# RWKV projection: value slabs last, and head sums as two rounded products

## The reference, cut to what matters

```python
rkvg = einsum('bsmd,mde->bsme', xs[:, :, :4], w_in)     # xs = h + xx * mu, one mix per matrix
r, k, v, g = rkvg[:, :, 0], rkvg[:, :, 1], rkvg[:, :, 2], rkvg[:, :, 3]
kk = heads(k * k_k)
kk = kk / maximum(sqrt(sum(kk * kk, axis=-1)), 1e-12)     # key norms: sums over a head
k_dir = k * (1 + (icl - 1) * k_a)                         # icl: a sigmoid, for two directions
bonus = (sum(r * k_dir * r_k, axis=-1) * v).sum(over both directions)
out = ((groupnorm(scan(r, decay, k_dir, v, kk, icl)) + bonus) * silu(g)) @ w_out
```

## Time and profile before

| what | value |
|---|---|
| median of three runs | 4685.58 us |
| the profiled execution | 4690.08 us |
| its span, first to last instruction | 4688.3 us |
| TensorE matmul busy | 4258.9 us, 91% |
| VectorE, ScalarE busy | 2696.7 us, 58%; 1887.8 us, 40% |
| mean granted TensorE clock | 0.968 |
| DMA | 480.77 MB, mean 103 GB/s |

### The profile page before, as it was taken

The page is one execution under the profiler, slowest core; times in us unless marked ns, Lnnn a source line. Parts: engine busy times, 40 slices in busy tenths (PEclk is TensorE's granted clock), DMA queues, the critical chain, the costliest instruction groups (busy, mean ns, idle before and its releaser), DMA issues. The chain is left out here.

```text
span 4688.3 us, 137401 instructions
## 1 busy us (share of the span) xinstructions
PE 4258.9 (91%) x61184; PEld 3665.6 (78%) x61184; DVE 2696.7 (58%) x4665; ACT 1887.8 (40%) x3496; POOL 4.6 (0%) x10
## 2 busy tenths in 40 slices
PE   6999979999997899999998999889999789999978
PEld 2888768888885799766668899877988678888858
DVE  5433547777775654355556433466425577777755
ACT  5333225545554432355554000154332245555542
POOL 0000000000000000000000000000000000000000
PEclk8999989999999999899999999999999899999989
DMA  7444773333325132100000221112446733333341
GB/s 294 150 123 123 223 225 87 98 83 97 87 80 192 63 84 56 51 1 2 1 10 28 95 95 68 57 52 82 117 139 195 236 110 89 98 85 96 85 183 63
DMA packets 542442, 480.77 MB, mean 103 GB/s; under 512 B 29344, under 2 KB 500640, under 8 KB 534176
## 3 DMA queue, kind: packets, MB, share of 16 engines
q1 hardware_dynamic: 411040, 405.91, 27.3%
q10 hardware_dynamic: 130816, 66.07, 5.2%
HBM read 337.94 MB, written 128.71 MB: 100 GB/s over the span
## 5 line engine op out<-in xcount | busy, mean ns | idle before, releaser
L647 PE MATMUL ps<-big_r,stage_r 128*128 128x384 f32 x2976 | 641.3, 350 | 19.1 <-DVE big_r L908 17.7
L647 PEld LDWEIGHTS ps<-big_r,stage_r 128*128 128x128 f32 x2976 | 522.6, 190 | 75.7 <-issue 27.0
L2508 PE MATMUL ps<-big_r,w_out 128*128 128x384 f32 x2304 | 417.8, 341 | 36.5 <-DVE w_out L2624 36.2
L2508 PEld LDWEIGHTS ps<-big_r,w_out 128*128 128x128 f32 x2304 | 407.7, 191 | 44.9 <-DVE w_out L2624 39.2
L647 PE MATMUL ps<-big_r,w_slab_r 128*128 128x384 f32 x1488 | 341.4, 337 | 0.0
L370 PE MATMUL ps<-big_r,stage_r 128*128 128x384 f32 x1536 | 311.7, 337 | 13.2 <-DVE big_r L357 13.2
L2230 DVE TENSOR_REDUCE extra<-ps 128x1 f32<-128x1152 f32 (+1 forms) x144 | 177.6, 1234 | 205.0 <-PE ps L2135 205.0
L370 PEld LDWEIGHTS ps<-big_r,stage_r 128*128 128x128 f32 x1536 | 270.7, 189 | 27.7 <-issue 26.7
L1491 ACT COPY arena<-ps 128x512 f32<-128x512 f32 x288 | 168.9, 587 | 253.4 <-PE ps L1294 252.9
L647 PEld LDWEIGHTS ps<-big_r,w_slab_r 128*128 128x128 f32 x1488 | 268.2, 189 | 0.0
L1645 DVE COPY_PREDICATED arena<-arena,ps 128x128 f32<-128x128 uint32 x720 | 192.9, 325 | 116.6 <-PE ps L1282 115.5
(11 more groups left out here) (259 smaller groups left out, 8087.5 us busy)
## 6 DMA issues: line engine op xcount, KB each, us to landing
w_slab<-in_w SPq DMA_DIRECT2D x138, 512.0 KB, 3.7
scan_in<-x_resid ACTq DMA_DIRECT2D x112, 576.0 KB, 5.9
arena<-scan_in SPq DMA_DIRECT2D x144, 320.0 KB, 3.8
arena<-scan_in SPq DMA_DIRECT2D x288, 128.0 KB, 3.8
arena<-scan_in SPq DMA_DIRECT2D x48, 576.0 KB, 7.5
arena<-scan_in SPq DMA_DIRECT2D x144, 192.0 KB, 4.0
arena<-in_w_ada SPq DMA_DIRECT2D x24, 1024.0 KB, 5.8
x_resid<-in_w_ada SPq DMA_DIRECT2D x24, 1024.0 KB, 4.9
```

Source lines behind the costliest of these rows:

```text
L647: mm = pe.matmul(g.ps[:, 3 * s + c, 0:CW], w[:, k * P:(k + 1) * P], x[:, k, chunk(c)], start=k == i == 0, stop=k == NB - 1 and i == 2)
L2508: mm = pe.matmul(g.ps[:, bank(i, b), 0:wide[i]], w[:, b, k * P:(k + 1) * P], r, start=k == j == 0, stop=k == NB - 1 and j == 2)
```

## The change

The matrices' order becomes keys, receptance, gate, values: GATE = 18 and VAL = 26. The gate's sigmoid, product and store move to slabs 18 to 25. Values are the last matrix; the bonus is multiplied with the values in their copy buffer (evac), and the loads of values from memory are gone. Squares and bonus products are split into a high and a low part, and each norm and each sum is two rounded products with head_ones_r, a rounded copy of the ones. The norm of block 6 moves from slab 9 to slab 10. The first load of lora_up moves from the start to slab 12, since its place now holds the high squares. The last bonus block is copied, and multiplied by one instruction once the last values are out.

```diff
-RWKV_MATS = (..., ("value", 2, NB), ("gate", 3, NB))
+RWKV_MATS = (..., ("gate", 3, NB), ("value", 2, NB))
...
+    sq_high, sq_low = up_flat_r[:, 0:T], g.x_r[:, 4, :]
-    back = [[g.big[1][:, 2 + 3 * i + k, :] for k in range(3)] for i in range(2)]
+    back = [[g.big[1][:, 2 + 3 * i + k, :] for k in range(2)] for i in range(2)]
+    prod_low = [g.extra_r[:, 0:T], g.big_r[0][:, 0, :]]
+    prod_high = [g.big_r[1][:, 4 + 3 * i, :] for i in range(2)]
+    copies = lambda n: n + 1 if n < GATE else n + 1 - NB
...
@@ SP
-            def load_v(b):
-                sp.wait_ge(stored[b % 2], 16 * (9 + b // 2))
-                ...
-                sp.dma_start(tiled(back[b % 2][2]), blocks(b, A_V)).then_inc(v_in[b % 2], 16)
...
             def load_up(w):
                 if w:
                     sp.wait_ge(rate_mm, 2 * CH * NB)
+                else:
+                    sp.wait_ge(norm_mm, CH * NB)
...
-            load_up(0)
...
+                if n == RCP + 2:
+                    load_up(0)
+                if GATE < n <= VAL:
+                    store_gate(n - GATE - 1)
-                if n == GATE:
+                if n == VAL:
                     load_kr(0)
-                    load_v(0)
-                    slab(GATE + 2)
+                    slab(VAL + 2)
                     load_kr(1)
-                    load_v(1)
-                elif n > GATE:
-                    b = n - GATE
+                elif n > VAL:
+                    b = n - VAL
                     if b + 1 < NB:
                         load_kr(b + 1)
-                    store_gate(b - 1)
-                    if b + 1 < NB:
-                        load_v(b + 1)
                     store_bonus(b - 1)
                     if b == 4:
                         scan_head()
...
@@ TensorE
             def slab(n, m, between):
                 pe.wait_ge(low_ok, n - 2)
-                if n > GATE + 1:
-                    pe.wait_ge(silu_ok, n - GATE - 1)
+                if GATE <= n - 2 < VAL:
+                    pe.wait_ge(silu_ok, n - 2 - GATE + 1)
                 else:
-                    pe.wait_ge(copied, n - 1)
+                    pe.wait_ge(copied, copies(n - 2))
...
             def norm(b, c):
                 if c == 0:
-                    pe.wait_ge(sq_ok, b + 1)
+                    pe.wait_ge(sq_low_ok, b + 1)
...
-                pe.matmul(..., g.head_ones[:, :], sq[:, chunk(c)], start=True, stop=True).then_inc(norm_mm, 1)
+                pe.matmul(out, g.head_ones_r[:, :], sq_high[:, chunk(c)], start=True, stop=False)
+                pe.matmul(out, g.head_ones_r[:, :], sq_low[:, chunk(c)], start=False, stop=True).then_inc(norm_mm, 1)
...
             def sums(b, c):
                 if c == 0:
-                    pe.wait_ge(p_ok, b + 1)
+                    pe.wait_ge(p_low_ok, b + 1)
...
-                pe.matmul(..., g.head_ones[:, :], prod[b % 2][:, chunk(c)], start=True, stop=True).then_inc(sum_mm, 1)
+                pe.matmul(out, g.head_ones_r[:, :], prod_high[b % 2][:, chunk(c)], start=True, stop=False)
+                pe.matmul(out, g.head_ones_r[:, :], prod_low[b % 2][:, chunk(c)], start=False, stop=True).then_inc(sum_mm, 1)
...
-                if n < RCP - 1 or n == RCP + 1:
-                    q = min(n - KEY - 1, NB - 1)
+                if n < RCP - 1 or n in (RCP, RCP + 1):
+                    q = n - KEY - 1 if n < RCP else n - RCP + NB - 2
                     between = {4: (lambda q=q: norm(q, 0), lambda q=q: norm(q, 1)), 6: (lambda q=q: norm(q, 2),)}
-                elif n == RCP - 1:
-                    between = {2: (lambda: norm(NB - 2, 0), lambda: norm(NB - 2, 1)), 6: (lambda: norm(NB - 2, 2),)}
...
@@ ScalarE
             def copy_out(n):
                 act.wait_ge(proj_done, n + 1)
-                if n >= KEY + 2:
+                if n in (VAL, VAL + 1):
+                    act.wait_ge(silu_st[b % 2], 64)
+                elif n >= VAL:
+                    act.wait_ge(stored[n % 2], 16 * (NB + b // 2))
+                    act.wait_ge(bonus_ok, CH * (b - 1))
+                elif n >= KEY + 2:
                     act.wait_ge(stored[n % 2], 16 * (n // 2 - 1))
...
             def square(b):
                 A.activation(sq, evac[b % 2], ACT.Square, scale=ch(g, "k_k", 8 * j + b)).then_inc(sq_ok, 1)
+                A.activation(sq_high, evac[b % 2], ACT.Square, scale=ch(g, "k_k", 8 * j + b)).then_inc(sq_high_ok, 1)
...
-                copy_out(VAL + b)
+                gate(b)
             for b in range(NB):
                 if b < NB - 1:
                     for c in range(CH):
                         rates(NB + b + 1, c)
                         if b == c == 0:
-                            high_slab_of(GATE + 1)
-                gate(b)
+                            high_slab_of(VAL + 1)
+                act.wait_ge(p_ok, b + 1)
+                A.copy(prod_high[b % 2], prod[b % 2]).then_inc(p_high_ok, 1)
+                copy_out(VAL + b)
             for s in range(2):
                 act.wait_ge(rate_st[s], 16 * 16)
+                act.wait_ge(stored[s], 16 * 12)
...
@@ VectorE
             def bonuses(b, c):
-                    dve.wait_ge(v_in[b % 2], 16 * (b // 2 + 1))
...
+                out, sums = bonus[b % 2][:, chunk(c)], g.ps[:, bank(("sum", b, c)), 0:CW]
+                if b == NB - 1:
+                    V.tensor_copy(out, sums).then_inc(bonus_ok, 1)
+                    return
+                if c == 0:
+                    dve.wait_ge(copied, copies(VAL + b))
+                V.tensor_tensor(out, sums, evac[b % 2][:, chunk(c)], op=ALU.mult).then_inc(bonus_ok, 1)
...
+            def low_products(b):
+                dve.wait_ge(p_high_ok, b + 1)
+                V.tensor_tensor(prod_low[b % 2], prod[b % 2], prod_high[b % 2], op=ALU.subtract).then_inc(p_low_ok, 1)
+
+            def low_squares(b):
+                dve.wait_ge(sq_ok, b + 1)
+                dve.wait_ge(sq_high_ok, b + 1)
+                V.tensor_tensor(sq_low, sq, sq_high, op=ALU.subtract).then_inc(sq_low_ok, 1)
+
+            V.tensor_copy(g.head_ones_r[:, :], g.head_ones[:, :]).then_inc(ones_ok, 1)
...
                 if b == NB - 1 and m < 5:
-                    if m == 2:
-                        ... (transition(m + 1, keys_between); unit_keys(NB - 2))
+                    if m < 4:
+                        transition(m + 1, lambda k: None)
+                    else:
+                        def gate_between(k):
+                            if k == 2:
+                                gated(NB - 2)
+                        transition(m + 1, gate_between)
+                        gated(NB - 1)
                     continue
                 if m == 5:
                     if b:
                         rate_sums(b)
                     weighted_keys(b)
                     if b:
-                        gated(b - 1)
                         high_slab_of(n + 1)
                     products(b)
                     if b:
                         for c in range(CH):
                             bonuses(b - 1, c)
+                    low_products(b)
                     continue
                 if b:
                     high_slab_of(n + 1)
+                if m == 4 and b:
+                    gated(b - 1)
...
-                if KEY < n < RCP or n == RCP + 1:
-                    q = min(n - KEY - 1, NB - 1)
+                if KEY < n < RCP or n in (RCP, RCP + 1):
+                    q = n - KEY - 1 if n < RCP else n - RCP + NB - 2
+                    low_squares(q)
                     for c in range(CH):
                         maxima(q, c)
                     unit_keys(q)
...
-            gated(NB - 1)
-            dve.wait_ge(silu_ok, NB)
+            dve.wait_ge(copied, copies(W_RWKV - 1))
+            V.tensor_tensor(bonus[1], bonus[1], evac[1], op=ALU.mult).then_inc(last_ok, 1)
```

More of the change, by code:

```diff
@@ L401 @@
 ADA_WITH = ((1, 2, 3), (), (4, 5), ())
-RWKV_MATS = (("decay", 4, 1), ("rate", 5, 1), ("key", 1, NB), ("receptance", 0, NB), ("value", 2, NB), ("gate", 3, NB))
+RWKV_MATS = (("decay", 4, 1), ("rate", 5, 1), ("key", 1, NB), ("receptance", 0, NB), ("gate", 3, NB), ("value", 2, NB))
 def phase_rwkv_project(nc, g, layer, j):
@@ L432, in phase_rwkv_project @@
     first = [0, 1, 2, 10, 18, 26]
-    KEY, RCP, VAL, GATE = first[2:]
-    raw = lambda n: g.slab[:, n % 2] if n < GATE + 2 else g.big[0][:, 3 + n % 2, 0:D]
+    KEY, RCP, GATE, VAL = first[2:]
+    copies = lambda n: n + 1 if n < GATE else n + 1 - NB
+    raw = lambda n: g.slab[:, n % 2] if n < VAL + 2 else g.big[0][:, 3 + n % 2, 0:D]
     turned = [first[m] + i for m in (3, 4, 5) for i in range(2)]
@@ L438, in phase_rwkv_project @@
     V, A = nc.vector, nc.scalar
-    rates_in = dict(zip([*range(RCP + 3, RCP + 7), *range(VAL + 1, VAL + 5), VAL + 6], range(NB + 1)))
-    rates_in.update({GATE + b: NB + b + 1 for b in range(NB - 1)})
+    rates_in = dict(zip([*range(RCP + 3, RCP + 7), *range(GATE + 1, GATE + 5), GATE + 6], range(NB + 1)))
```

(19 more changed lines are left out.)

67 lines of the change are left out of this document (28 added, 39 removed).

## The result

| | median us | runs | ratio to before, 95% interval |
|---|---|---|---|
| before | 4686.63 (4680.41 to 4693.78) | 6 | |
| after | 4715.53 (4706.04 to 4721.80) | 6 | 1.0059 [1.0049, 1.0069] |
| forecast | 4680.6, range 4660 to 4702 | | 0.9989 |

The change made the kernel slower, by 28.9 us, and the time lies outside the range. The profiled execution of after took 4709.96 (span 4708.1).

What follows compares the result with a forecast made beforehand. TensorE was taken to bound the projections, hardly resting outside a few slabs. Terms summed to -2.5 us a phase, -5.0 for two: 4680.6 against the median of 4685.6, with an 8-in-10 range of 4660 to 4702.

Steps and rivals of the forecast that it cites:

- Slab 27: Gate store ahead of key and receptance loads makes them late: +2.3 us a phase, bounds 0 and +7.
- Slabs 3 to 8: Key norms as two rounded products gain 0.93 us a slab, -5.6 a phase; second square and subtraction fit in time.
- Slab 32: Rates wait for the rate store's landing, sooner with less traffic ahead: -6 us a phase, bounds 0 and -10.
- Rival C: The rate store's share of the engines is fixed, so slab 32's wait stays: +7 us, 4693; chance 0.12.
- Slabs 28 to 31: Loop over ScalarE's rounded copy and VectorE's low products sets 17.0 us a slab: -1.1 a phase, bounds -0.98 and +1 each.
- Rival B: ScalarE's queue, now issuing value stores too, becomes the bound in the last stage: +17 us, 4703; chance 0.12.
- slabs 9 and 10: Block 6's norm waits in slab 10 for the transition; TensorE rests 8.6 us, then slower clock: +9.7 a phase.
- Slabs 11: Cheaper norms -0.93 us, low squares some 0.2 late: -0.7 a phase.
- 26: Gate product added to the transition, last matrix's slab perhaps sooner: +0.4 us a phase, bounds -1 and +1.4.
- 33: Six cheaper sums, none behind the loop: -1.9 us a phase; the phase's ends +0.4, bounds -0.5 and +3.
- Rivals A: Queue relief is worth more: slab 32 falls to 17.0 in both phases, slab 27 gains 1 us: 4665; chance 0.18.
- D: The wait in slab 10 isn't there: -24 us, 4661; chance 0.04.

Runs made afterwards that it cites:

- the mended version: After with low squares ahead of the split, block 6's norm mostly in slab 9, gate store behind key loads: 0.9960, again 0.9980; with unrounded sums 0.9978.

## Why the prediction was wrong

The forecast was -5.0 for two phases and they took +28.1. Of the 33 between them:

- **Slab 27, 13.4 of it.** The mechanism was the forecast one, a store moved past loads; the term of +2.3 was mis-sized (+6.9 / +11.1), and in phase 2 its upper bound of +7 too. Counted from slab 27's start, with before's slab at 506.20 and after's at 514.6, the loads went out at 503.6 (forecast 503.5) and VectorE had them at 511.4 (forecast 510), TensorE resumed at 519.7 (518.2): 1.5 of it. The larger part is the second block, for which the forecast had "about 1.5 more". Its loads were in place 13.0 us after their issue began, where the forecast took 6.5 for a landing, while everything SP had held back was under way on full DMA engines (1.09, 322 GB/s); TensorE rested again 3.88. The rests are the loss: 4.31 us before, 7.61 and 3.88 after. The half clock behind a rest, which I priced for slabs 10 and 32 and not here, is not: before has it in slab 27 too (0.86 in the earlier trace rows), and TensorE was busy 2.9 us beyond a slab's own pace before (20.19 less 17.28) and 3.4 after (19.81 less 16.38). In phase 2 the issue and the landing were slower still (VectorE waited 8.73 and 3.69). Moving the store back took 18.0 away.
- **Slabs 3 to 8, 10.0.** The price of a norm was right: 0.93 a slab, 0.91 in slab 8 and in the 82.0 of the run with the squares first. The step that failed is "fit": the forecast let the low squares end at 6.8, from ScalarE's copy and squares and the subtraction alone, and did not list what stands ahead of the subtraction on VectorE, whose queue has 4.5 us of halving and split there. The sentence "up to 1 if they were late" held the outcome and went into neither the term nor the range.
- **Slab 32, 6.7.** Phase 1 gave 5.3 of 6; phase 2 gave nothing. From the issue of the rate store to the sigmoids that wait for it were 16.6 and 13.6 us; now 12.8 (613.55 to 626.35) and 14.4. The forecast took 5.5 from both; 3.8 came in phase 1, and 0.8 was lost in phase 2. The engines were full in this wait (1.10, 349 GB/s), so 4.5 MB passed in it, the store's own 1.18 MB among them, and which of the others the store had to let pass is not seen in a row. The run without value stores (23.7 / 24.9) says that the 0.59 MB of a value store behind it matter by under 1 us, as far as one run tells. Rival C, the fixed share, fits phase 2 and not phase 1. The Trainium skill's rule behind it (DMA: Bandwidth & Descriptors, Queues, rings and completion order: turns packet by packet between the rows that have work) was not isolated by any run here. Why the phases differ stays open.
- **Slabs 28 to 31, 4.5.** The loop was wrongly named. It is not the copy, the low products and the sums (the forecast's 17.0, and it is some 0.3 us from being the one that ends last) but the rate store's landing: 8.11 and 9.14 are 17.25. The 17.3 that TensorE itself needed before (and in the run with the sums back) are as long as that loop, so it could not be seen there, and making the sums cheaper than it could not give anything. Of the 4.5, 2.6 are slab 29, where the landing came later than in its neighbours (9.06 for 8.11 in phase 1); why is open. Rival B named the right place, ScalarE's queue in the last stage, but the issue pair took 1.02 to 1.05 in slabs 28 to 30 of both phases, 1.65 and 1.28 in slab 31, and over 2 only at the start of slab 27 in phase 2 (2.32): in slabs 28 to 31 its mechanism isn't there.

Right were slabs 9 and 10: forecast TensorE's restart 32.2 after slab 9's start, measured 32.3; rest 8.6, measured 8.4; whole stretch 40.9, measured 40.2. Slabs 11, 12 to 25, 26 and 33 came out within 0.6 of their terms, but for slab 26 in phase 2 (1.6 better). Rivals A and D are refuted: slab 32 did not fall to 17, and the wait in slab 10 is there.

The range failed with the terms. The text had upper bounds of +7 for slab 27, 0 for slab 32, 1 late in each of slabs 3 to 8 (+0.4) and +1 each in 28 to 31. They add up to 21.8 a phase above the terms, 4724 for the whole, and the result lies inside that. The range of 4702 reached to rival B, which had slabs 28 to 31 and slab 32 at these bounds and slab 27 at +1 above its term; slabs 3 to 8 coming late, and the rest of slab 27's bound, it left out. And three of the four share the crowded transfers of the last stage, so they could be expected to come together.

## What to carry to other kernels

A cheaper product is worth at most what lies between TensorE's pace and the next loop that takes nearly as long: measure the loop's turn (issue to issue of its store) before crediting the product. When an instruction is added to an engine, write down what stands ahead of it in that engine's order, also where it has time by its inputs. And a store moved ahead of loads in one queue delays every later load, so price the second pair as well as the first.

## What was not expected of the hardware

- A pair of loads (keys and receptance) took 1.0 to 1.6 us to issue where SP had been idle before it, and 2.46 to 6.21 behind other commands in slab 27, so that the commands behind it were issued late.
- A rate store let go of its buffer after 8.1 us at 241 GB/s, and after 12.8 at 349 GB/s: more bytes moved a microsecond, and the landing came later.
- After a rest of 8.36 us the granted clock was 0.50 for some microseconds, and a rounded product took 0.52 for 0.33. After rests of about 2 us in slab 29 it was one or the other: with 2.40 (after, phase 2) the slab took 18.96 at granted clock 1.00, with 1.81 (low squares ahead, phase 2) 19.89, with a stretch at 0.50. After rests of 0.6 to 1.75 in slabs 28 to 31 it never fell.
- With unrounded sums slab 29 took 19.5 and 17.3 in the mended version, with rests of 2.0 and 0, with rounded ones 20.6 and 20.6 (18.3 and 20.3 in its other run), with rests of 1.7 to 2.5: the version that needs TensorE less waits as long there or longer. Which transfers collide was not settled.
